# Both ends of a hybrid attention and DeltaNet block: a third buffer for the input norm, its first 512 tokens in feature halves, and the last outputs written in place

## The reference, cut to what matters

```python
def rms_norm(x, g):
    y = x * lax.rsqrt(jnp.mean(jnp.square(x), axis=-1, keepdims=True) + EPS)
    return y * g
h = rms_norm(x, norm_mix_g)
proj = h @ w_in            # q, k, v, indexer, DeltaNet columns
...
return rms_norm(x, norm_final_g)
```

## Time and profile before

| what | us |
|---|---|
| median of 3 runs | 3906.88 |
| lowest and highest of them | 3900.57, 3912.32 |
| the profiled execution, its own time | 3907.71 |
| its span, first to last instruction | 3905.9 |
| PE busy in the span | 3443.3 (88%) |
| mean granted TensorE clock | 0.945 of full |

### The profile page before, as it was taken

The page is one execution under the profiler, slowest core; times in us unless marked ns, Lnnn a source line. Parts: engine busy times, 40 slices in busy tenths (PEclk is TensorE's granted clock), DMA queues, the critical chain, the costliest instruction groups (busy, mean ns, idle before and its releaser), DMA issues.

```text
span 3905.9 us, 47540 instructions
## 1 busy us (share of the span) xinstructions
PE 3443.3 (88%) x16994; PEld 2814.0 (72%) x16994; DVE 2044.3 (52%) x3568; ACT 2165.9 (55%) x3717; POOL 1382.1 (35%) x721
## 2 busy tenths in 40 slices
PE   7799967888888894679999889999899999999998
PEld 5688856677777773467777668787677878867886
DVE  5224036777777753546455475757466575433222
ACT  4212137666745553476967869695877944433222
POOL 4110043434254433324443334333333333334442
PEclk9899978999999997699999999999999999999999
DMA  3511161413233233423333343333343333342222
GB/s 112 207 68 65 65 158 53 111 56 74 96 88 84 72 116 105 120 93 104 105 107 118 105 139 107 114 111 111 108 125 116 110 106 98 96 135 87 97 92 75
DMA packets 318058, 401.25 MB, mean 103 GB/s; under 512 B 25968, under 2 KB 241136, under 8 KB 313200
## 3 DMA queue, kind: packets, MB, share of 16 engines
q1 hardware_dynamic: 313072, 366.75, 31.3%
q10 hardware_dynamic: 4752, 31.46, 2.1%
HBM read 327.43 MB, written 70.68 MB: 102 GB/s over the span
## 4 chain that ended last, share of the span: by engine, by line
PE 31%; ACT 14%; DVE 7%; issue 4%; POOL 2%; DMA 2%; SPq 1%; ACTq 0%; DVEq 0%; POOLq 0%
PE m_ps L2060 8%; PE m_ps L2062 8%; PE m_ps L2061 8%; ACT m_junk L1778 6%; ACT m_wh L1836 2%; PE m_ps L2150 2%; PE m_ps L2138 2%; POOL m_wl L1723 1%; ACT m_prob L1863 1%; ACT m_verdict L1780 1%; ACT m_trial L1784 1%; PE m_ps L2123 1%; PE m_ps L2124 1%; PE m_ps L2103 1%; ACT m_phi L1852 1%
## 5 line engine op out<-in xcount | busy, mean ns | idle before, releaser
L1723 POOL TENSOR_TENSOR m_wl<-m_raw,m_wh 128x1024 fp32r<-128x1024 f32 x288 | 721.0, 2503 | 1397.2 <-ACT m_wh L1836 1397.2
L2060 PE MATMUL m_ps<-m_ah,m_wh 128*128 128x512 f32 x1280 | 530.2, 414 | 41.3 <-DVE m_al L1920 30.7
L2062 PE MATMUL m_ps<-m_ah,m_wl 128*128 128x512 f32 x1280 | 508.0, 397 | 0.0
L2061 PE MATMUL m_ps<-m_al,m_wh 128*128 128x512 f32 x1280 | 507.2, 396 | 0.0
L2060 PE MATMUL m_ps<-m_th,m_wh 128*128 128x512 f32 x1024 | 426.8, 417 | 39.8 <-DVE m_tl L1905 22.8
L2062 PE MATMUL m_ps<-m_th,m_wl 128*128 128x512 f32 x1024 | 406.4, 397 | 0.0
L2061 PE MATMUL m_ps<-m_tl,m_wh 128*128 128x512 f32 x1024 | 406.0, 396 | 0.0
L1778 ACT ACTIVATE m_junk<-m_sc,m_trial 128x1152 int8<-128x1152 f32 (+7 forms) x248 | 401.6, 1619 | 4.7 <-DVE m_sc L2020 3.3
L1836 ACT ACTIVATE m_wh<-m_raw 128x1024 fp32r<-128x1024 f32 x288 | 302.7, 1051 | 138.8 <-PE m_ps L2062 123.5
L2060 PEld LDWEIGHTS m_ps<-m_ah,m_wh 128*128 128x128 f32 x1280 | 245.3, 192 | 102.1 <-DVE m_al L1920 33.0
L1852 ACT ACTIVATE m_phi<-m_ps 128x512 fp32r<-128x512 f32 (+1 forms) x288 | 164.3, 571 | 263.5 <-PE m_ps L2138 259.6
(11 more groups left out here) (311 smaller groups left out, 7569.5 us busy)
## 6 DMA issues: line engine op xcount, KB each, us to landing
m_raw<-w_units SPq DMA_DIRECT2D x288, 512.0 KB, 3.6
m_vals<-valsT SPq DMA_DIRECT2D x256, 128.0 KB, 3.6
p_raw<-w_proj SPq DMA_DIRECT2D x72, 256.0 KB, 4.1
projT<-work ACTq DMA_DIRECT2D x12, 1024.0 KB, 3.8
g_qkvz<-projT SPq DMA_DIRECT2D x16, 768.0 KB, 5.5
wraw<-w_proj SPq DMA_DIRECT2D x21, 512.0 KB, 3.5
projT<-p_out SPq DMA_DIRECT2D x36, 256.0 KB, 3.2
work<-xT SPq DMA_DIRECT2D x8, 1024.0 KB, 5.5
```

The lines of the kernel that those rows point to most:

```text
L1723: nc.gpsimd.tensor_tensor(wl[:, n % 3, :], raw[:, n % 2, :], wh[:, n % 3, :].bitcast(fp32), ALU.subtract).then_inc(w_lo, 1)
L2060: nc.tensor.matmul(dst, hi, rh, start=first, stop=False)
L2061: nc.tensor.matmul(dst, hi, r_low, start=False, stop=False)
L2062: return nc.tensor.matmul(dst, lo, rh, start=False, stop=last)
```

## The change

In the first part: `xb` gets a third buffer, which lies in the half of `stage` that chunk 0 fills later; the load of block b waits for block b-3. The first load of x is cut into two DMAs of 4 feature pieces each, the load of block 2 goes ahead of the second weight chunk, and the load of `cw` goes behind it. For blocks 0 and 1 (b < FINE = 2) the squares, the sums, the norm, the rounded copy and the low part are signalled in halves of 512 features: ACT squares and rounds two halves, and of the low part POOL makes the first half and DVE the second, behind its norm of block 1. POOL's low part of the second weight chunk goes behind these. ACT's order is written anew: after a hand-ordered start, for each b from 2 on, square of b+2, root of b+1, rounded copy of b. PE projects one chain per sum one block earlier: chain b-2 behind the sum of block b.

In the last part: for the last block of 512 tokens, DVE writes its 8 outputs over `acc` and SP stores them from there, so no output waits for a store.

```diff
--- before.py
+++ after.py
@@ -92,8 +92,10 @@
         xh, xl = blocks_of(xh, "xh"), blocks_of(xl, "xl")
         normed = lambda part, b: part[b * XB // 512][:, :, b * XB % 512:b * XB % 512 + XB]
         work = sb("work", [P, 8192])
-        xb = work[:, 0:4096].rearrange("p (u k s) -> p u k s", u=2, k=KC)
-        xsq = work[:, 4096:6144].rearrange("p (k s) -> p k s", k=KC)
+        tile_at = lambda i: work[:, i * KC * XB:(i + 1) * KC * XB].rearrange("p (k s) -> p k s", k=KC)
+        xb = [tile_at(0), tile_at(1), stage[:, 0, HALO:HALO + KC * XB].rearrange("p (k s) -> p k s", k=KC)]
+        xsq = tile_at(2)
+        FINE, HALVES = 512 // XB, (slice(0, KC // 2), slice(KC // 2, KC))
         conv_acc = work[:, 0:2 * S].rearrange("p (u s) -> p u s", u=2)
         conv_out = work[:, 2 * S:4 * S].rearrange("p (u s) -> p u s", u=2)
         rstd = sb("rstd", [P, 2, XB])
@@ -108,7 +110,8 @@
         ps = ctx.enter_context(nc.psum_tensor("ps", [P, 8, 512], fp32))
         const_in, const_set = sem("const_in"), sem("const_set")
         pair = lambda n: [sem(f"{n}{u}") for u in range(2)]
-        x_in, w_in = map(pair, ["x_in", "w_in"])
+        x_in, w_in = [sem(f"x_in{u}") for u in range(3)], pair("w_in")
+        x_half, sq_half, ss_half, xn_half, xh_half, xl_half = map(sem, ["x_half", "sq_half", "ss_half", "xn_half", "xh_half", "xl_half"])
         split_kept, shared_in = sem("split_kept"), sem("shared_in")
         sq_done, ss_done, log_done, rstd_done, xn_done, xh_done, xl_done = map(
             sem, ["sq_done", "ss_done", "log_done", "rstd_done", "xn_done", "xh_done", "xl_done"])
@@ -123,9 +126,13 @@
         @block.sync
         def _(sp):
             def x_load(b):
-                if b >= 2:
-                    sp.wait_ge(xn_done, b - 1)
-                sp.dma_start(xb[:, b % 2, :, :], xT[:, :, tokens(b)]).then_inc(x_in[b % 2], 16)
+                if b >= 3:
+                    sp.wait_ge(xn_done, b - 2)
+                if b == 0:
+                    sp.dma_start(xb[0][:, HALVES[0], :], xT[:, HALVES[0], tokens(0)]).then_inc(x_half, 16)
+                    sp.dma_start(xb[0][:, HALVES[1], :], xT[:, HALVES[1], tokens(0)]).then_inc(x_in[0], 16)
+                else:
+                    sp.dma_start(xb[b % 3], xT[:, :, tokens(b)]).then_inc(x_in[b % 3], 16)
 
             def w_load(c):
                 if c >= 2:
@@ -134,11 +141,12 @@
 
             x_load(0)
             sp.dma_start(gm[:, :], a["g_mix"]).then_inc(const_in, 16)
-            sp.dma_start(cw[:, :, :], a["conv_w"]).then_inc(const_in, 16)
             x_load(1)
             w_load(0)
+            x_load(2)
             w_load(1)
-            for b in range(2, NX):
+            sp.dma_start(cw[:, :, :], a["conv_w"]).then_inc(const_in, 16)
+            for b in range(3, NX):
                 x_load(b)
             for n in SHARED:
                 sp.dma_start(shared[n][:, :], a[n]).then_inc(shared_in, 16)
@@ -150,6 +158,8 @@
                 b = c - 4
                 if 0 <= b < NB and b != FIRST_LATER:
                     sp.wait_ge(xl_done, 512 // XB * (b + 1))
+                    if b == 0:
+                        sp.wait_ge(xl_half, FINE)
                     for kept, part in ((xhT, xh), (xlT, xl)):
                         sp.dma_start(kept[b], part[b].bitcast(fp32)).then_inc(split_kept, 16)
             sp.wait_ge(split_kept, 32 * (NB - 1))
@@ -169,11 +179,13 @@
                                         ALU.subtract).then_inc(w_lo, 1)
 
             split_lo(0)
-            split_lo(1)
             for b in range(NX):
-                pool.wait_ge(xh_done, b + 1)
-                nc.gpsimd.tensor_tensor(normed(xl, b), xn[b % 2], normed(xh, b).bitcast(fp32),
+                pool.wait_ge(xh_half if b < FINE else xh_done, b + 1)
+                part = HALVES[0] if b < FINE else slice(0, KC)
+                nc.gpsimd.tensor_tensor(normed(xl, b)[:, part, :], xn[b % 2][:, part, :], normed(xh, b)[:, part, :].bitcast(fp32),
                                         ALU.subtract).then_inc(xl_done, 1)
+                if b == FINE - 1:
+                    split_lo(1)
             for c in range(2, N):
                 split_lo(c)
 
@@ -185,11 +197,19 @@
                 dve.wait_ge(rstd_done, b + 1)
                 if b >= 2:
                     dve.wait_ge(xl_done, b - 1)
+                    dve.wait_ge(xl_half, min(b - 1, FINE))
                 for k in range(KC):
                     last = nc.vector.scalar_tensor_tensor(
-                        out=xn[b % 2][:, k, :], in0=xb[:, b % 2, k, :], scalar=gm[:, k:k + 1], in1=rstd[:, b % 2, :],
+                        out=xn[b % 2][:, k, :], in0=xb[b % 3][:, k, :], scalar=gm[:, k:k + 1], in1=rstd[:, b % 2, :],
                         op0=ALU.mult, op1=ALU.mult)
+                    if b < FINE and k == KC // 2 - 1:
+                        last.then_inc(xn_half, 1)
                 last.then_inc(xn_done, 1)
+                if b == FINE - 1:
+                    for i in range(FINE):
+                        dve.wait_ge(xh_done, i + 1)
+                        nc.vector.tensor_tensor(normed(xl, i)[:, HALVES[1], :], xn[i][:, HALVES[1], :],
+                                                normed(xh, i)[:, HALVES[1], :].bitcast(fp32), ALU.subtract).then_inc(xl_half, 1)
             for k in range(N_CONV):
                 c = conv_at[k]
                 u = c % 2
@@ -209,21 +229,19 @@
         @block.scalar
         def _(act):
             def square(b):
-                act.wait_ge(x_in[b % 2], 16 * (b // 2 + 1))
+                if b == 0:
+                    act.wait_ge(x_half, 16)
+                    nc.scalar.activation(xsq[:, HALVES[0], :], xb[0][:, HALVES[0], :], ACT.Square).then_inc(sq_half, 1)
+                act.wait_ge(x_in[b % 3], 16 * (b // 3 + 1))
+                if b == 1:
+                    act.wait_ge(ss_half, 1)
+                    nc.scalar.activation(xsq[:, HALVES[0], :], xb[1][:, HALVES[0], :], ACT.Square).then_inc(sq_half, 1)
                 if b:
                     act.wait_ge(ss_done, b)
-                nc.scalar.activation(xsq[:, :, :], xb[:, b % 2, :, :], ACT.Square).then_inc(sq_done, 1)
-
-            def split_hi(c):
-                act.wait_ge(w_in[c % 2], 16 * (c // 2 + 1))
-                if c >= 2:
-                    act.wait_ge(acc_done, chain_at[c - 2, last_of(c - 2)] + 1)
-                nc.scalar.activation(wh[:, c % 2, :, :], wraw[:, c % 2, :, :], ACT.Copy).then_inc(w_hi, 1)
-
-            nc.scalar.preload_act_table_set("natural_log_exp_and_others")
-            act.wait_ge(const_set, 3)
-            square(0)
-            for b in range(NX):
+                part = HALVES[1] if b < FINE else slice(0, KC)
+                nc.scalar.activation(xsq[:, part, :], xb[b % 3][:, part, :], ACT.Square).then_inc(sq_done, 1)
+
+            def root(b):
                 act.wait_ge(ss_done, b + 1)
                 if b >= 2:
                     act.wait_ge(xn_done, b - 1)
@@ -231,12 +249,40 @@
                                      bias=eps_col[:, :]).then_inc(log_done, 1)
                 act.wait_ge(log_done, b + 1)
                 nc.scalar.activation(rstd[:, b % 2, :], rstd[:, b % 2, :], ACT.Exp, scale=-0.5).then_inc(rstd_done, 1)
+
+            def high(b):
+                if b < FINE:
+                    act.wait_ge(xn_half, b + 1)
+                    nc.scalar.activation(normed(xh, b)[:, HALVES[0], :], xn[b % 2][:, HALVES[0], :], ACT.Copy).then_inc(xh_half, 1)
+                act.wait_ge(xn_done, b + 1)
+                part = HALVES[1] if b < FINE else slice(0, KC)
+                nc.scalar.activation(normed(xh, b)[:, part, :], xn[b % 2][:, part, :], ACT.Copy).then_inc(xh_done, 1)
+
+            def split_hi(c):
+                act.wait_ge(w_in[c % 2], 16 * (c // 2 + 1))
+                if c >= 2:
+                    act.wait_ge(acc_done, chain_at[c - 2, last_of(c - 2)] + 1)
+                nc.scalar.activation(wh[:, c % 2, :, :], wraw[:, c % 2, :, :], ACT.Copy).then_inc(w_hi, 1)
+
+            nc.scalar.preload_act_table_set("natural_log_exp_and_others")
+            act.wait_ge(const_set, 3)
+            square(0)
+            square(1)
+            root(0)
+            split_hi(0)
+            root(1)
+            high(0)
+            square(2)
+            high(1)
+            split_hi(1)
+            root(2)
+            square(3)
+            for b in range(2, NX):
+                if b + 2 < NX:
+                    square(b + 2)
                 if b + 1 < NX:
-                    square(b + 1)
-                if b < 2:
-                    split_hi(b)
-                act.wait_ge(xn_done, b + 1)
-                nc.scalar.activation(normed(xh, b), xn[b % 2], ACT.Copy).then_inc(xh_done, 1)
+                    root(b + 1)
+                high(b)
 
             for c, (kind, chunk, k, blocks) in enumerate(kinds):
                 u = c % 2
@@ -266,10 +312,14 @@
         @block.tensor
         def _(pe):
```

(62 more changed lines are left out.)

## The result

The changed kernel takes 3916.36 us (median; 3910.28 to 3923.49), the kernel before 3905.23 over all its runs beside it: ratio 1.0025, 95% interval 1.0018 to 1.0031, 11.1 us slower or 0.28%. Forecast were +13.3 us, with 0.32 on "within 0.3%" and 0.62 on "slower by more". The profiled execution of the changed kernel took 3923.49 us, 7.1 above its median; that of before stood 2.5 above its own. One profiled execution of one experiment (`two_buf`) ran throughout at a granted clock of 0.55 and took 5746.1 us; it is left out, and a second trace of that kernel is used.

A forecast was written before the change was run, and what follows sets the result against it. PE is busy 88% of the span, but the change touches only the ends, and all later work hangs on chain 6. Front +18.2 and tail -4.9 make +13.3 us: 3920.2 us against 3906.88, range 3909 to 3927.

The forecast's parts named there:

- Two waits of 9.5 us from the two orders together: Chains 2 and 4, behind sums 4 and 6: PE idles 9.5 us each until POOL's low part, 19.0 in all.
- The last stretch: From the end of sum 7 to chain 6, through root, copies, norm 7 and POOL's low part: 15.3 us, 14.1 before.
- Start of chain 0: PE's first chain starts at 31.9 instead of 43.96, after DVE's second half difference, held by POOL's weight split, ends at 31.8.
- Low clock: PE slows after idling: 2.4 us lost after each long wait (1.6 to 3.2), 1.0 at chain 0 (0 to 2.9).
- Sums: Five PE sums of squares between chain 0 and chain 6 at 3.72 us each, 18.6 us in all.
- `cw` at 17.9 and DVE's first norm at 18.0: Start: the taps land at about 17.9 behind more x, so DVE's norm starts at 18.0, 2.1 us after before's 15.90.
- The tail: Last block's outputs in place: three store waits go, 5.2 us less 0.3 for queueing, -4.9 us (-4.0 to -5.2).
- The third buffer is hidden anyway: Input loads at the front: x is in place before ACT asks, so the third buffer was given no gain.
- smaller prices: Rival, chance 0.09: same two waits, `cw` earlier, chain 0 at 30, clock losses 1.6 each; +7.9 us, 3914.8.
- The clock does not come back: Rival, chance 0.05: PE's sums 3, 5 and 7 take 6.0 to 6.7 us instead of 3.72; +8, 3928.
- The early start pays in full: Rival, chance 0.06: PE is fed without the two waits from 33 on, chain 6 at 84.2, total 3884.

The follow-up runs named there:

- two_buf: `both_cw` with two input buffers instead of three; 3900.04 us, ratio 0.9987 to the kernel before.
- pe_later: The changed kernel with PE taking chain b-3 behind sum b again; 3884.94 us, ratio 0.9945 to the kernel before.
- copy_first: The changed kernel with ACT making the rounded copy of b ahead of square b+2 and root b+1; 3900.26 us, ratio 0.9987 to the kernel before.
- both_cw: The changed kernel with chain b-3 behind sum b, ACT's copy first and `cw` loaded right behind the gains; 3889.74 us, ratio 0.9958 to before.
- pe_cw: `pe_later` with `cw` loaded right behind the gains, ahead of the second block of x; 3886.40 us, ratio 0.9945 to the kernel before.
- change_two: The changed kernel with two input buffers instead of three, taps still behind the weights; 3936.85 us, ratio 1.0075 to the kernel before.
- pool_low: The changed kernel with POOL making both low-part halves of blocks 0 and 1, DVE none; 3923.14 us, ratio 1.0046 to the kernel before.
- front_only: The changed kernel with the last block's outputs again through the two halves of tmp; 3921.38 us, ratio 1.0040 to the kernel before.
- pe_later_2: `pe_later` run once more, beside `pe_cw`; 3886.53 us, ratio 0.9941 to the kernel before.

## Why the prediction was right, and where it was not

The range held the time, the direction and the cause were right, and the median came out 3.8 us under the forecast. Of that 1.6 is that before's median, over more runs, is 3905.23 and not 3906.88; the other 2.2 put the change just inside 0.3% instead of just outside, so that not the likelier "slower by more" came, but the 0.32. That it is no more than 2.2 is in part luck: the two ends of the trace make +9.1 of the 13.3, and the 2 us that they do not explain bring the medians nearer to the forecast. By its own steps:

- **Two waits of 9.5 us from the two orders together.** Measured 9.42 and 9.42. `pe_later` and `copy_first` each take one of the two orders away and remove 9 and 5.6 us of each: shown.
- **The last stretch, 15.3 us from sum 7 to chain 6.** Measured 94.90 + 3.61 = 98.51 to 113.74, 15.2.
- **Start of chain 0, 31.9 (bounds 30 to 33).** Measured 29.97, the lower bound. Some 1.2 of the 1.9 us are DVE's start, 16.67 and not 18.0 (its first instruction was held 0.16 us). The rest is the chain of holds, which went another way: norm 1 was not held by POOL's first half. It ran 20.00 to 23.24, and POOL, which had started at 19.66, took 6.92 us for 2.35 us of work; DVE's differences were done at 27.67, and POOL's half of block 1, at 26.55 + 3.33 = 29.88, was last. But who was held did not set the time: in `pe_later` DVE started at 16.63, norm 1 was held as forecast (20.11 to 25.46), and the last low part was done at 29.89. What the forecast had too long is the second difference, which it put behind the weight split, to 31.8; in `pe_later` it runs ahead of the split.
- **Low clock.** The 1.0 at chain 0 did not occur (0.47 us for its first matmul). Chain 2 took 64.90 - 57.46 = 7.44 and chain 4 94.90 - 86.98 = 7.92, 2.0 and 2.5 above 5.44; 2.4 was taken.
- **Sums.** Behind a chain they take 3.61, not 3.72: 0.5 over five.
- These terms make 117.8 - 113.7 = 4.1: 1.9 start, 1.0 clock at chain 0, 0.3 at the others, 0.5 sums, 0.3 waits and last stretch.
- **`cw` at 17.9 and DVE's first norm at 18.0.** Measured 16.67, and waiting for `cw`, so the wait was seen and 1.3 us over-sized. That it costs 2.1 us is more than the rows bear out. In `both_cw` and `pe_cw` the taps are early and the last low part is done at 28.86 and 28.92 instead of 29.88, so I estimate 1 us at chain 0; the changed kernel itself was not run with early taps.
- **The tail, -4.9.** Measured -5.3 in the trace, -4.3 +-4 by the runs. The stretches show 366 and 387 GB/s at a DMA share of 1.03 to 1.05, so the engines were full, and from the last output's end (3918.5) to the end it took 3.2 us against 2.9 (3903.0): the 0.3 for queueing was right. The eight outputs took 5.39 us, not 5.7.
- **"The third buffer is hidden anyway"**: wrong, as `change_two` and `two_buf` show. The step looked at when ACT asks for x with the buffer there, not at when the loads would land without it. It had no part in the sum, since the changed kernel has the buffer.

The rival *smaller prices* (3914.8) came nearer to the time, 1.6 us off against 3.8, and partly for its reasons: chain 0 at 30 at full clock. The taps were earlier than forecast, but DVE still waited for them, and its smaller clock losses (1.6) did not occur. *The clock does not come back* did not occur: sums 3, 5 and 7 took 3.61 to 3.62. *The early start pays in full* has its mechanism not here but in `pe_later`: PE fed without the long waits, chain 6 at 85.87 where it has 84.2.

By the Trainium skill, SBUF — State Buffer, section SBUF: two separate sides, whoever starts first holds the shared ports for its whole instruction. The rows agree that one engine stands still. They do not show that the first to start wins: as far as POOL's spans can be trusted (the profile calls them rough), its half started at 19.66, while the last instruction of norm 0 still ran (to 20.07), and DVE's norm 1 at 20.00; POOL was the one held, until DVE's ninth instruction from there ended at 24.4. In `pe_later` POOL started at 19.77 beside a norm 0 that ran to 20.19, as close, and went first. In the changed kernel it then ran to 26.58 and DVE's second difference, begun at 24.89, was held in turn.

## What to carry to other kernels

When two engines' orders are both written by hand, follow one item round the ring. Here PE put sum b ahead of the chain that needs copy b-1, and ACT put root b, which needs that sum, ahead of that copy: each order alone is harmless or half as dear, both together leave PE empty for 9.4 us a turn, and undoing the one on PE made 11 us of loss into 21 of gain. A buffer that looks idle in the trace that has it must be judged by the trace that would lack it. A constant loaded late that one engine waits for may cost nothing, if the stage behind it hangs on something else: in `pe_cw` chain 0 stood behind sum 3.

## What the runs showed that I had not expected

Two engines that hold each other up do not share the loss in a fixed way. POOL's first low half, the same instruction in the same place, took 6.92 us in the changed kernel and 5.81 in `pool_low`, but 2.63 in `front_only` and `pe_later`, with DVE held instead. It is not the program that decides: `pe_later_2` is the same kernel as `pe_later`. POOL in `pe_later`, then in `pe_later_2`:

```profile
19.77 2.63 POOL L185 TENSOR_TENSOR xl<-work,xh 128x1024 fp32r<-128x1024 f32 x1 [2.64 <-ACT xh L256]
```

```profile
19.63 6.93 POOL L185 TENSOR_TENSOR xl<-work,xh 128x1024 fp32r<-128x1024 f32 x1 [2.84 <-ACT xh L256]
```

DVE's norm 1 took 5.35 us in the first and 3.25 in the second. The last low part was done at 29.89 and at 26.52 + 3.33 = 29.85, so for the time it made no difference who lost.
